# Two weight rings with their own remainders modulo 512 bytes, and a value projection in steps of 512 channels, in a float32 encoder kernel

## The reference, cut to what matters

```python
h = rms_norm(x)
u = h @ W_in + b_in                 # q k v o z_a gates glu_a glu_b z_b g_a g_b
q, k = silu(depthwise_conv(q|k, 5 taps))
ht = mLSTM forward + mLSTM backward, 4 heads of 512 channels, from q, k, v and the gates
y_a = (norm(sigmoid(o) * ht) * silu(z_a)) @ W_a
c = depthwise_conv(glu_a * sigmoid(glu_b), 31 taps)
y_b = (silu(layer_norm(c)) * silu(z_b)) @ W_b
x = x + (sigmoid(g_a) * y_a + sigmoid(g_b) * y_b) @ W_out
```

## Time and profile before

| | |
|---|---|
| median of 3 runs | 2445.06 us (2444.18 to 2446.43) |
| the profiled execution | 2446.6 us, span 2444.6 us |
| TensorE matmul busy | 2423.7 us, 99%, 13,988 matmuls |
| VectorE busy | 1936.1 us, 79% |
| ScalarE busy | 1362.9 us, 56% |
| DMA | 444.9 MB, 60.8% of 16 engines' span |
| TensorE's granted clock, mean | 0.998 |

### The profile page before, as it was taken

One profiled execution on the slowest core, in us unless ns is written; L12 is line 12 of the kernel. 1 busy time (PEld: TensorE's weight loads), 2 busy tenths in 40 slices (PEclk: granted clock), 3 DMA queues, 4 the chain that ended last, 5 costly groups with the idle time before them and its releaser, 6 DMA issues.

```text
span 2444.6 us, 40470 instructions
## 1 busy us (share of the span) xinstructions
PE 2423.7 (99%) x13988; PEld 2126.6 (87%) x13988; DVE 1936.1 (79%) x2896; ACT 1362.9 (56%) x1632; POOL 41.9 (2%) x45
## 2 busy tenths in 40 slices
PE   7999999999999999999999999999999999999998
PEld 6888888888888888888888888888888888888887
DVE  7788989898987887556678888888888878765565
ACT  5655454545465557555566654545454655665554
POOL 1000000000000000000000000000000000000000
PEclk9999999999999999999999999999999999999999
DMA  7666656565656666665656665656565666666654
GB/s 208 174 194 178 180 168 182 168 182 168 184 177 188 195 184 189 191 192 182 199 151 197 195 188 167 182 168 181 168 181 163 194 186 195 177 197 193 189 189 139
DMA packets 448205, 444.90 MB, mean 182 GB/s; under 512 B 18000, under 2 KB 445792, under 8 KB 448096
## 3 DMA queue, kind: packets, MB, share of 16 engines
q1 hardware_dynamic: 448096, 443.74, 60.8%
HBM read 441.59 MB, written 2.10 MB: 181 GB/s over the span
## 4 chain that ended last, share of the span: by engine, by line
PE 93%; DVE 3%; issue 2%; ACT 1%; DVEq 0%; DMA 0%; SPq 0%; ACTq 0%
PE ps L1447 54%; PE ps L1450 27%; PE ps L1466 5%; PE ps L1468 2%; PE px L1628 1%; PE px L1607 1%; DVE W L778 1%; PE px L1519 0%; DVE HEAD L1094 0%; DVE HEAD L1209 0%; DVE EW L1109 0%; PE ps L1674 0%; PE px L1551 0%; ACT W L428 0%; ACT YC L634 0%
## 5 line engine op out<-in xcount | busy, mean ns | idle before, releaser
L1447 PE MATMUL ps<-Hs,W 128*128 128x512 f32 x4960 | 1547.9, 393 | 1.6 <-DVE W L778 1.6
L778 DVE TENSOR_TENSOR W<-RAW,W 128x1024 fp32r<-128x1024 f32 x832 | 1028.2, 1243 | 400.7 <-ACT W L428 398.6
L428 ACT CAST W<-RAW 128x1024 fp32r<-128x1024 f32 x832 | 863.3, 1049 | 810.7 <-PE ps L1450 686.5
L1450 PEld LDWEIGHTS ps<-Hs,W 128*128 128x128 f32 x4960 | 932.2, 188 | 205.6
L1450 PE MATMUL ps<-Hs,W 128*128 128x256 f32 x4960 | 979.8, 279 | 0.0
L1447 PEld LDWEIGHTS ps<-Hs,W 128*128 128x128 f32 x4960 | 753.2, 188 | 6.1 <-issue 5.1
L925 DVE SCALAR_TENSOR_TENSOR ACC<-CP,CWT,ACC 128x256 f32<-128x256 f32 x928 | 389.6, 482 | 0.4
L1447 PE MATMUL ps<-YC,W 128*128 128x512 f32 x1152 | 359.3, 393 | 4.8 <-DVE W L778 3.8
L1450 PEld LDWEIGHTS ps<-YC,W 128*128 128x128 f32 x1152 | 216.9, 188 | 47.8
L1450 PE MATMUL ps<-YC,W 128*128 128x256 f32 x1152 | 227.9, 279 | 0.0
L1466 PE MATMUL ps<-W,Hs 128*128 128x512 f32 x512 | 182.9, 400 | 0.0
(11 more groups left out here) (216 smaller groups left out, 995.1 us busy)
## 6 DMA issues: line engine op xcount, KB each, us to landing
RAW<-in_w_in_dram SPq DMA_DIRECT2D x640, 512.0 KB, 3.7
RAW<-in_w_a_dram SPq DMA_DIRECT2D x64, 512.0 KB, 3.4
RAW<-in_w_b_dram SPq DMA_DIRECT2D x64, 512.0 KB, 3.4
RAW<-in_w_out_dram SPq DMA_DIRECT2D x64, 512.0 KB, 4.1
M<-in_x_dram SPq DMA_DIRECT2D x2, 1024.0 KB, 7.7
HEAD<-in_b_in_dram SPq DMA_DIRECT2D x8, 256.0 KB, 4.1
out_dram<-M SPq DMA_DIRECT2D x4, 256.0 KB, 3.2
out_dram<-M SPq DMA_DIRECT2D x2, 512.0 KB, 4.7
```

The source lines that it names most:

```text
L428: nc.scalar.copy(WH[:, c, :, :], RAW[:, c, :, :]).then_inc(hi_made, 1)
L778: v.tensor_tensor(WL[:, c, :, :], RAW[:, c, :, :], WH[:, c, :, :].bitcast(F32), ALU.subtract).then_inc(lo_made, 1)
L1447: mm(ps[:, 2 * q + t, :], WH[:, c, kk, t * P:t * P + P], act_in[:, kt, :], start=(kt == 0), stop=False)
L1450: i = mm(ps[:, 2 * q + t, S:2 * S], WL[:, c, kk, t * P:t * P + P], act_in[:, kt, 0:S], start=False, stop=(kt == KT - 1))
```

## The change

`W`, 128 partitions x 4 chunks x 2 halves x 4 tiles x 256, is split in two tensors `WH` and `WL` of 4 x 4 x 256 each, with 16 unused floats between them. The value projection of a head is still two steps, but each takes all 512 channels of the head and half of the contraction: step 4 the contraction tiles 0 to 7, step 5 the tiles 8 to 15. A chunk is then 2 contraction tiles x 512 channels (the same 1024 floats per partition, seen through `RAWT`, `WHT` and `WLT`). Per tile there are six matmuls of 512 columns, three products for each half of the positions, all summed in banks 2 and 3 of `px`. They are drained once, after step 5, by one VectorE copy of 128x1024 into `VS`. ScalarE's `low_half` of steps 4 and 5 and VectorE's two `pair_out` go; their counts are made up by `act.sem_inc(low_out, 2)` and `dve.sem_inc(pairs_out, 1)`.

```diff
--- before.py
+++ after.py
@@ -48,6 +48,7 @@
 PAD = DW_TAPS // 2
 CW = S + PAD
 SKEW = 112
+LOW_SKEW = 16
 EPS = 1e-6
 NG = 4 * H
 GATE0 = 5 * D
@@ -128,7 +129,9 @@
         YC = sb("YC", [P, KT, 2 * S], F32R)
         sb("SKEW", [P, SKEW])
         RAW = sb("RAW", [P, QC, KQ, PC])
-        W = sb("W", [P, QC, 2, KQ, PC], F32R)
+        WH = sb("WH", [P, QC, KQ, PC], F32R)[:]
+        sb("LOW_SKEW", [P, LOW_SKEW])
+        WL = sb("WL", [P, QC, KQ, PC], F32R)[:]
         CP = sb("CP", [P, KT * CW + PAD])
         M = sb("M", [P, KT, S])
         HEAD = sb("HEAD", [P, KT, S])
@@ -156,7 +159,8 @@
         NW = sb("NW", [P, KT])
         GS = sb("GS", [P, KT, 2, NG], F32R)
 
-        WH, WL = W[:, :, 0, :, :], W[:, :, 1, :, :]
+        RAWT = RAW[:].rearrange("p c (a b) n -> p c a (b n)", a=2)
+        WHT, WLT = (w.rearrange("p c (a b) n -> p c a (b n)", a=2) for w in (WH, WL))
         K_, V_, SO_ = (HEAD[:, HT * i:HT * (i + 1), :] for i in (0, 2, 3))
         VS = V_.rearrange("p (s a) b -> p s (a b)", s=ST)
         VB = HEAD[:, HT:HT + 2, :].rearrange("p a b -> p (a b)")
@@ -313,6 +317,14 @@
                 for c in range(QC):
                     load_quarter(w, l, col, n, c)
 
+            def load_half(w, l, col, n, half):
+
+                for c in range(QC):
+                    k = half * (KT // 2) + 2 * c
+                    sp.wait_ge(lo_made, n * QC + (c + 1))
+                    sp.dma_start(RAWT[:, c, :, :], w[l, :, k:k + 2, ds(col, 2 * PC)]
+                                 ).then_inc(raw_in[c], 16)
+
             load_x(0)
             load_quarter(w_in_v, 0, GLU_A, 0, 0)
             load_x(1)
@@ -346,6 +358,10 @@
                     sp.dma_start(VB, b_in[l:l + 1, h * DH + V_T * P:h * DH + V_T * P + DH].partition_broadcast(P)
                                  ).then_inc(v_bias_in, 16)
                     for i, first in enumerate((K_T, Q_T, V_T, O_T, Z_T)):
+                        if first == V_T:
+                            load_half(w_in_v, l, h * DH + first * P, n + 2 * i, 0)
+                            load_half(w_in_v, l, h * DH + first * P, n + (2 * i + 1), 1)
+                            continue
                         load_pair(w_in_v, l, h * DH + first * P, n + 2 * i)
                         load_pair(w_in_v, l, h * DH + (first * P + PC), n + (2 * i + 1))
                 for j in range(0, N_GA // 2):
@@ -604,8 +620,10 @@
                         b = (K_, QB)[i // 2][:, 2 * (i % 2):2 * (i % 2) + 2, :]
                         nc.scalar.activation(b, b, ACT.Silu).then_inc(qk_silu, 1)
                         split_rest(n, i + 1)
-                        low_half(n, i + 1, None if first is None else bias(first))
-                    split_and_low(n, 5)
+                        if first is not None:
+                            low_half(n, i + 1, bias(first))
+                    split_rest(n, 5, 0)
+                    act.sem_inc(low_out, 2)
                     split_and_low(n, 6, bias(O_T))
                     split_rest(n, 7, 0, 1)
                     sigmoid_out(n, 6, SO_[:, 0:2, :], o_sig)
@@ -1124,7 +1142,7 @@
                     pair_out(n, 3, QPAD[:, :, 2:2 + S])
                     narrow_conv(3, QB[:, 2:4, :], 2)
                     with_taps(4, 3, 9)
-                    pair_out(n, 4, VS[:, :, 0:PC])
+                    dve.sem_inc(pairs_out, 1)
                     split_lo(n + 6, 0)
                     dve.wait_ge(scores, u + 1)
                     sc = px[:, 0, :].rearrange("p (a b) -> p a b", a=ST)
@@ -1144,7 +1162,8 @@
                     split_lo(n + 6, 2)
                     conv_taps(duo, 13, 15)
                     split_lo(n + 6, 3)
-                    pair_out(n, 5, VS[:, :, PC:2 * PC])
+                    dve.wait_ge(multiplied, n * QC + 7 * QC)
+                    v.tensor_copy(VS, px[:, 2:4, :]).then_inc(pairs_out, 1)
 
                     split_lo(n + 7, 0)
                     dve.wait_ge(dens, u + 1)
@@ -1451,22 +1470,21 @@
                                    act_in[:, kt, 0:S], start=False, stop=(kt == KT - 1))
                     i.then_inc(multiplied, 1)
 
-            def multiply_turned(n, k):
-
-
-                q = k % 2
+            def multiply_turned(n, k, half):
+
+
                 for c in range(QC):
                     pe.wait_ge(lo_made, n * QC + (k * QC + QC + c + 1))
                     if c == 0:
                         pe.wait_ge(pairs_out, n + (k + 1))
-                    for kk in range(KQ):
-                        kt = c * KQ + kk
-                        for s in range(ST):
-                            bank = ps[:, 2 * q + s, :].rearrange("p (a b) -> p a b", a=2)
-                            mm(bank, Hs[:, kt, s * P:(s + 1) * P], W[:, c, :, kk, :],
-                               start=(kt == 0), stop=False)
-                            i = mm(bank[:, 1, :], Hs[:, kt, S + s * P:S + (s + 1) * P],
-                                   W[:, c, 0, kk, :], start=False, stop=(kt == KT - 1))
+                    for kk in range(2):
+                        kt = half * (KT // 2) + 2 * c + kk
+                        for low_x, low_w in ((0, 0), (0, 1), (1, 0)):
+                            for s in range(ST):
+                                at = low_x * S + s * P
+                                i = mm(px[:, 2 + s, :], Hs[:, kt, at:at + P], (WHT, WLT)[low_w][:, c, kk, :],
+                                       start=(kt == 0 and low_x + low_w == 0),
+                                       stop=(kt == KT - 1 and low_x == 1))
                     i.then_inc(multiplied, 1)
 
 
@@ -1600,14 +1618,14 @@
                        start=True, stop=True).then_inc(m_spread, 1)
                     for k in range(1, 4):
                         multiply(n, k, Hs)
-                    multiply_turned(n, 4)
+                    multiply_turned(n, 4, 0)
                     pe.wait_ge(qk_silu, u * 4 + 4)
                     for s in range(ST):
                         for k in range(HT):
                             i = mm(px[:, 0, s * S:(s + 1) * S], K_[:, k, s * P:(s + 1) * P],
                                    QB[:, k, :], start=(k == 0), stop=(k == HT - 1))
                     i.then_inc(scores, 1)
-                    multiply_turned(n, 5)
+                    multiply_turned(n, 5, 1)
 
                     pe.wait_ge(pw_summed, u + 1)
                     for d in range(2):
```

## The result

| | before | changed |
|---|---|---|
| median | 2445.14 us (2444.18 to 2446.43, 4 runs) | 2472.47 us (2470.92 to 2473.02, 4 runs) |
| profiled execution, span | 2446.6, 2444.6 us | 2473.0, 2471.3 us |
| ratio | | 1.0108 (1.0096 to 1.0120) |

The change makes the kernel slower by 1.1%, 27 us. The forecast was 2430 with a range from 2410 to 2454: wrong in sign and outside the range. The second rival, that the low loads collide, had said 2470.

What follows compares the result with a forecast made beforehand. TensorE's intervals between matmuls were taken to bound the kernel. From the profiled 2446.6 us, 12.3 (moving WL) and 2.4 (value projection) gave 2431.9, less 1.5 to the median: 2430 us, range 2410 to 2454.

Steps and rivals of the forecast that it cites:

- The second rival: Ordinary steps: low-tile loads at the moving tile's remainder disturb it, costing 25 us, value steps gain nothing; 2470 us, chance 0.19.
- What bounds the kernel: TensorE, busy 99% of the span: the time is the sum of intervals between matmuls, longest waits only 12.3 us.
- Part 1: Low weights WL moved by 64 bytes to remainder 0: ordinary groups of four matmuls 0.004 us shorter, a gain of 12.3 us.
- the sign goes by two rows: Gain on ordinary steps inferred from the varying low pair and from f32 matmuls with equal remainders showing no excess.
- the f32 rows: Profile rows of plain f32 256-column matmuls, both operands at one remainder: 0.2156 us each, taken as showing no excess.
- The bound below: Most the WL move could gain in ordinary steps: 0.01 us off the low pair in 3072 groups, 31 us.
- the bound above: Most the WL move could lose in ordinary steps: 0.008 us in each of 3072 groups, 25 us.
- the turned form: Old value projection, stationary and moving swapped so weights stream: 0.353 us per pair against 0.345 for the same columns.
- Part 2: Value projection, 48 matmuls of 512 columns a step instead of 64: 0.15 us less in 16 steps, 2.4 us gained.
- Beside TensorE: Work on other engines and transfers: one 1.2 us VectorE copy replaces two sums, nobody waits, nothing added to the time.
- Addresses don't matter: Rival on ordinary steps: WL's remainder has no effect, only the value projection's 2.4 us counts; 2443 us, chance 0.28.

Runs made afterwards that it cites:

- e4: Changed kernel without SKEW and without the gap between WH and WL, so both lie at the activations' remainder 0 (modulo 512 bytes): 2456.16 us.
- v1: Kernel before, with its old value steps, only the low half of W moved to remainder 0 and the high half kept at 448: 2467.32 us.
- b1: Changed kernel without the 64 bytes between WH and WL, both at remainder 448, new value steps kept, timed closely: 2444.39 us, ratio 0.9996.
- g1: Changed kernel, but the 256-column matmuls of ordinary steps load tiles from WH instead of WL, for timing only: 2441.36 us.
- e2: Changed kernel without the 64 bytes between WH and WL, both at remainder 448, the same kernel as b1, run once: 2443.46 us.

## Why the prediction was wrong

**What bounds the kernel: right.** Only the intervals moved; no wait did.

**Part 1, wrong in sign.** The step that failed is the sentence "the sign goes by two rows". The first reading was that the low pair is what varies between groups (0.22 and 0.24), so that its loads are what the placement disturbs, so that another place helps. But the group's sum hardly moves with it: by the starts in that trace to the nanosecond it is 0.693 and 0.687 by turns, so the high pair takes back half of what the low pair gives. Even with every group at 0.687 the gain would be 0.003 x 3072 = 9 us, not 31, and no run had a chunk below the 2.76 that these two sums give. An interval that varies around a nearly constant sum shows where slack is shifted, not that there is any to gain. The second reading carried the f32 rows, 0.2156 us with both operands at one remainder, over to f32r. `e4` tried that equality for ordinary steps: 2.79 us, worse than 2.76. For the value steps equality is the best that was seen, 10.90 us. So the same pair of remainders is good with weights streaming and bad with activations streaming, and the f32 rows could decide neither. In place of the 12.3 us gained the ordinary steps lost 29.7. The bound below, 31 us of gain, had no ground; the bound above, 25 us of loss, came near by luck. It took the turned form's 0.353 as the price of a bad placement, but `v1` has that form faster, 11.11 in place of 11.29, with the low half at 0.

**Part 2, right in size, wrong in cause.** -0.15 us a step was forecast, -0.185 measured; the size was luck. `v1` shows that the old value steps gain as much from the low half at 0 alone. The new form by itself gives 0.09 a step (`b1`). In the changed kernel it gives nothing on top.

**Beside TensorE, right.** The copy took 1.22 us for an estimated 1.2 and started as long after the step's end as the sum did. GpSimd's addition took 3.32 us in that head where it took 2.40, which nobody waited for. The transfers land in 3.7 us as before.

**The rivals.** *Low loads collide* had the cause right (`g1`) and a chance of only 0.19. Its time was within 3 us partly by luck: 25 us for 29.7, against nothing for the 3.0 that the value steps gained. Its place was half right, since the matmuls during which high tiles are loaded got longer too. *Addresses don't matter* fell: `e2` against the changed kernel differs by 64 bytes and 29 us. The Trainium skill (TensorE: Matmul & The Clock Gate, Part 2: What happens when you issue a matmul) says that loading the next tile's weights takes no read bandwidth from the running matmul. The f32r runs here don't bear out that such a load is free: `g1` differs from the changed kernel only in which tiles the low matmuls of the ordinary steps load, and by 31 us.

**What stays open.** How a load and a moving tile disturb each other, and whether it is the distance between them that counts, since no run moved the activations from 0. The runs show a period of 256 bytes, costs that don't add, and, with the high ring at 448 and the low one at 0, three levels (2.79, 2.80, 2.83) at one of which the stream can stay for a whole stage. That looks like two streams locking at one of several offsets, and the small matmuls between the steps would choose it. No run changed that offset alone, so it is only argued.

## What to carry to other kernels

Where TensorE is the bound and its matmuls stream f32r, the addresses of the tiles modulo 256 bytes can be worth 1 to 2% (2443 to 2484 us here for the same instructions), and they can be moved for 64 bytes of padding. Sweep them for each form of matmul separately. A different remainder for each chunk of a ring shows four in one run, but the neighbours shift a chunk by up to 0.03 us, as much as the places do, so compare the candidates with all chunks at one place. Don't reason out the best place from which tiles are equal: here that was right for one form and wrong for the other.

## What was not expected of the hardware

In the new value steps a matmul of 512 columns in f32r took between 0.2271 us (all operands at one remainder, `e4`) and 0.2333 (`e2`) at granted clocks of 0.998 and 0.999, by the place of its operands alone. Two placements that each cost time alone, 15 and 29 us, cost 13 together. And the same instructions on the same tiles ran at 2.80 us a chunk in `v1` and at 2.83 in the changed kernel for a whole stage of some 160 us, and at 2.79 in the changed kernel later on.
